# Head norms of both tiles in step, filler products in four waits of TensorE, and the last value tiles of a half evicted by two engines ahead of a weight split

## The reference

```python
h = rmsnorm_2(x, attn_norm)
qkv = h @ w_qkv                       # a: three groups of q, k, v; b: one; 16 heads of 64
q = rope(rmsnorm(q) * q_gain)         # norm over the 64 numbers of a head, for every head
k = rope(rmsnorm(k) * k_gain)
p = exp(q @ k.T * scale + mask - max) # dilated bands in a, causal in b
x = x + (p @ v / sum(p)) @ w_o
hn = rmsnorm_2(x, ffn_norm)
x = x + (silu(conv(hn @ w_gate)) * conv(hn @ w_val)) @ w_down
```

## Time and profile before

| what | value |
|---|---|
| median of 3 runs | 1156.03 us (1153.71 to 1156.86) |
| the profiled execution's own time | 1157.73 us |
| its span in the trace | 1155.9 us |
| PE busy | 1115.3 us, 96% of the span |
| PEld, DVE, ACT, POOL busy | 84%, 68%, 56%, 1% |
| chain that ended last | PE 87%, DVE 6%, ACT 5%, issue 2%, DMA 1% |
| mean DMA rate | 159 GB/s |

### The profile page before, as it was taken

The page is one execution under the profiler, slowest core; times in us unless marked ns, Lnnn a source line. Parts: engine busy times, 40 slices in busy tenths (PEclk is TensorE's granted clock), DMA queues, the critical chain, the costliest instruction groups (busy, mean ns, idle before and its releaser), DMA issues.

```text
span 1155.9 us, 19015 instructions
## 1 busy us (share of the span) xinstructions
PE 1115.3 (96%) x6928; PEld 969.3 (84%) x6928; DVE 788.3 (68%) x1435; ACT 646.7 (56%) x1122; POOL 12.9 (1%) x22
## 2 busy tenths in 40 slices
PE   7998789999998999999999999999999999999998
PEld 5876679998987887888878999999876769999997
DVE  5767566555557667576674687787874746887776
ACT  5364455454456555655575665555666556655554
POOL 0000100000000000000000000000000000000000
PEclk9997689999999999999999999999999999999999
DMA  9552045655644655046541456556552515565562
GB/s 324 149 182 73 26 132 183 189 182 186 193 147 148 213 180 165 25 147 203 161 146 46 156 184 208 190 168 195 169 177 74 185 56 179 182 199 182 165 203 106
DMA packets 117037, 184.33 MB, mean 159 GB/s; under 512 B 6640, under 2 KB 70384, under 8 KB 116720
## 3 DMA queue, kind: packets, MB, share of 16 engines
q1 hardware_dynamic: 116688, 183.23, 50.0%
q10 hardware_dynamic: 288, 0.29, 0.1%
HBM read 182.45 MB, written 1.05 MB: 159 GB/s over the span
## 4 chain that ended last, share of the span: by engine, by line
PE 87%; DVE 6%; ACT 5%; issue 2%; DMA 1%; SPq 0%; DVEq 0%; ACTq 0%
PE ps L679 10%; PE ps L681 10%; PE ps L680 10%; PE ps L655 10%; PE ps L657 9%; PE ps L656 9%; PE ps L738 5%; PE ps L739 5%; PE ps L740 5%; PE ps L832 2%; PE ps L815 2%; PE ps L797 2%; ACT w_hi L1117 1%; PE ps L858 1%; PE ps L755 1%
## 5 line engine op out<-in xcount | busy, mean ns | idle before, releaser
L1624 DVE TENSOR_TENSOR w_lo<-w_stage,w_hi 128x1024 fp32r<-128x1024 f32 x336 | 403.1, 1222 | 191.3 <-ACT w_hi L1117 190.4
L1117 ACT ACTIVATE w_hi<-w_stage 128x1024 fp32r<-128x1024 f32 x336 | 347.7, 1053 | 182.7 <-PE ps L657 86.6
L679 PE MATMUL ps<-aT_hi,w_hi 128*128 128x256 f32 x992 | 282.2, 284 | 0.7 <-DVE aT_lo L1638 0.7
L680 PE MATMUL ps<-aT_lo,w_hi 128*128 128x256 f32 x992 | 281.2, 283 | 0.0
L681 PE MATMUL ps<-aT_hi,w_lo 128*128 128x256 f32 x992 | 281.2, 283 | 0.0
L655 PE MATMUL ps<-w_hi,aT_hi 128*128 128x512 f32 x480 | 194.2, 405 | 3.9 <-DVE w_lo L1697 2.2
L679 PEld LDWEIGHTS ps<-aT_hi,w_hi 128*128 128x128 f32 x992 | 190.8, 192 | 2.3 <-issue 1.0
L680 PEld LDWEIGHTS ps<-aT_lo,w_hi 128*128 128x128 f32 x992 | 190.9, 192 | 1.0
L681 PEld LDWEIGHTS ps<-aT_hi,w_lo 128*128 128x128 f32 x992 | 190.8, 192 | 0.0
L657 PE MATMUL ps<-w_hi,aT_lo 128*128 128x512 f32 x480 | 190.1, 396 | 0.0
L656 PE MATMUL ps<-w_lo,aT_hi 128*128 128x512 f32 x480 | 190.0, 396 | 0.0
(11 more groups left out here) (220 smaller groups left out, 1165.9 us busy)
## 6 DMA issues: line engine op xcount, KB each, us to landing
w_stage<-in_ffn_w_up SPq DMA_DIRECT2D x88, 512.0 KB, 4.7
w_stage<-in_a_w_qkv SPq DMA_DIRECT2D x72, 512.0 KB, 4.1
w_stage<-in_ffn_w_down SPq DMA_DIRECT2D x44, 512.0 KB, 3.5
w_stage<-in_w_up SPq DMA_DIRECT2D x32, 512.0 KB, 3.8
w_stage<-in_w_down SPq DMA_DIRECT2D x32, 512.0 KB, 4.2
w_stage<-in_w_in SPq DMA_DIRECT2D x24, 512.0 KB, 4.7
w_stage<-in_b_w_qkv SPq DMA_DIRECT2D x24, 512.0 KB, 4.5
w_stage<-in_w_out SPq DMA_DIRECT2D x8, 512.0 KB, 3.8
```

What stands on the lines that cost most here:

```text
L679: pe.matmul(o, wh, aT_hi[:, k, :], start=(k == 0), stop=False)
L680: pe.matmul(o, wh, aT_lo[:, k, :], start=False, stop=False)
L1117: act.activation(w_hi[:, slot, :], w_in[:, slot, :], ACT.Copy).then_inc(hi_done[slot], 1)
L1624: dve.tensor_tensor(w_lo[:, slot, :], w_in[:, slot, :], w_hi[:, slot, :].bitcast(F32), ALU.subtract).then_inc(lo_done[slot], 1)
```

## The change

Three parts.

- `head_norms` is split in two. ACT squares both token tiles back to back (`head_squares`), with the fourth split of the quarter group behind the squares, and then takes one Ln and one Exp over 16 columns for both tiles (`head_scales`). DVE sums both (`head_means`) and later scales and rotates both (`rotated_heads`). On ACT both norms now stand ahead of the eviction of q. On DVE split 7 moves behind the rotations of k. On PE the transposes of k in the last group stand behind v tile 3 instead of 4, and v tiles 6 and 7 behind the scores of unit 1.
- `spin` issues plain fp32 products of 128 by 128 columns into a bank that is written anew afterwards: 8 on a tile of zeros and 2 and 10 on the identity around the first transposes, 13 at the end of `mix`, 16 and 10 ahead of the two late `turn_x`. POOL clears the tile of zeros first.
- At the end of a half ACT takes the exponentials of unit 1 and evicts v's token tile 0 ahead of split 11, DVE evicts token tile 1 ahead of its split 11.

```diff
...
+            def spin(n, o, m):
+                for _ in range(n):
+                    pe.matmul(o, m, m, start=True, stop=True)
+            pe.wait_ge(s["zeroed"], 1)
+            spin(8, ps[:, 3, 0:P], hid[:, 0, 0:P])
             pe.wait_ge(s["ident_in"], 16)
             for ks in (LOW, HIGH):
                 for t in range(TOK):
                     turn_x("norm_in1", in_ready, t, ks)
+                    if (t, ks) == (0, LOW):
+                        spin(2, ps[:, 3, 0:P], ident)
+            spin(10, ps[:, 3, 0:P], ident)
...
+            pe.wait_ge(*is_drained(S_, f"sA{2 * NH1 - 1}"))
+            spin(13, ps[:, 0, 0:P], ident)
             pe.wait_ge(s["osq"], at(S_, "osq", 3))
...
             last_rows(S_, 4, "r3", 1, range(5, KT))
+            spin(16, ps[:, 7, 0:P], ident)
             turn_x("norm_mlp", ready, 1, LOW)
...
             last_down(S_, 0, range(4), ((1, 1),), True)
+            spin(10, ps[:, 7, S:2 * S].rearrange("p (r t c) -> p r t c", t=TOK, c=8)[:, :, 1, :], ident)
             turn_x("norm_a", ready, 1, LOW, "in")
...
-                        dense_rows(S_, 0, n + 8, v, tiles=range(KT - 3))
+                        dense_rows(S_, 0, n + 8, v, tiles=range(KT - 4))
                         turn_heads(S_, (f"kt{g}0", f"kt{g}1"), 0, 4 * g + 4)
-                        dense_rows(S_, 0, n + 8, v, tiles=[KT - 3])
+                        dense_rows(S_, 0, n + 8, v, tiles=[KT - 4])
                         for nm in (f"kt{g}0", f"kt{g}1"):
                             pe.wait_ge(*is_drained(S_, nm))
-                        for u in range(2):
-                            scores(S_, units[u], u)
-                            dense_rows(S_, 0, n + 8, v, tiles=[KT - 2 + u])
+                        scores(S_, units[0], 0)
+                        dense_rows(S_, 0, n + 8, v, tiles=[KT - 3])
+                        scores(S_, units[1], 1)
+                        dense_rows(S_, 0, n + 8, v, tiles=range(KT - 2, KT))
...
-                def head_norms(names):
+                def head_squares(names):
...
-                        act.wait_ge(s["ms8"], at(S_, "ms8", n[0], i))
-                        rsqrt(stat(f"rs8{t}", 8), stat(f"ms8{t}", 8), stat(f"ln8{t}", 8), "rs8")
+                def head_scales():
+                    act.wait_ge(s["ms8"], at(S_, "ms8", n[0], i))
+                    rsqrt(stat("rs8", 16), stat("ms8", 16), stat("ln8", 16), "rs8")
                 for g in range(groups):
                     q0 = g * 12
-                    splits(S_, range(q0, q0 + 4), i)
-                    head_norms((f"q{g}0", f"q{g}1"))
-                    splits(S_, range(q0 + 4, q0 + 8), i)
+                    splits(S_, range(q0, q0 + 3), i)
+                    head_squares((f"q{g}0", f"q{g}1"))
+                    split(S_, q0 + 3, i)
+                    head_scales()
+                    splits(S_, range(q0 + 4, q0 + 7), i)
+                    head_squares((f"k{g}0", f"k{g}1"))
+                    split(S_, q0 + 7, i)
+                    head_scales()
                     for j in range(2):
                         evac_q(...)
-                    head_norms((f"k{g}0", f"k{g}1"))
...
                     if last:
                         split(S_, q0 + 10)
                         exps(S_, units[0], 0)
-                    splits(S_, range(q0 + 11, q0 + 12), i)
-                    for t in range(TOK):
-                        evac_v(S_, f"v{g}{t}", i, vv[:, t, g * 512:(g + 1) * 512], stat("rtok", 2)[:, t:t + 1])
+                        exps(S_, units[1], 1)
+                        evac_v(S_, f"v{g}0", i, vv[:, 0, g * 512:(g + 1) * 512], stat("rtok", 2)[:, 0:1])
+                        split(S_, q0 + 11)
...
             def _(pool):
+            pool.memset(hid[:, 0, :], 0.0).then_inc(s["zeroed"], 1)
...
             def project_heads(S_, i, groups, layer, units):      # DVE
...
-                    splits(S_, range(q0, q0 + 4), i)
+                    splits(S_, range(q0, q0 + 3), i)
+                    head_means((f"q{g}0", f"q{g}1"))
+                    split(S_, q0 + 3, i)
...
-                    head_norms((f"q{g}0", f"q{g}1"), 0, (layer * 3 + g) * 2)
-                    splits(S_, range(q0 + 4, q0 + 8), i)
+                    rotated_heads((f"q{g}0", f"q{g}1"), (layer * 3 + g) * 2)
+                    splits(S_, range(q0 + 4, q0 + 7), i)
+                    head_means((f"k{g}0", f"k{g}1"))
                     for j in range(2):
                         dve.wait_ge(*is_full(S_, f"qt{g}{j}", i))
-                    head_norms((f"k{g}0", f"k{g}1"), 1, (layer * 3 + g) * 2 + 1)
+                    rotated_heads((f"k{g}0", f"k{g}1"), (layer * 3 + g) * 2 + 1)
+                    split(S_, q0 + 7, i)
...
                 maxima(S_, units[1], 1)
+                last = f"v{groups - 1}1"
+                b = bank(S_, last)
+                dve.wait_ge(*is_full(S_, last))
+                dve.tensor_scalar(vv[:, 1, (groups - 1) * 512:groups * 512], ps[:, b, :], stat("rtok", 2)[:, 1:2], None,
+                                  ALU.mult).then_inc(drained[b], 1)
                 split(S_, q0 + 11)
```

More of the change, by code:

```diff
@@ L257, in make_plan @@
     halves_a = [Stage(f"half_a{n}", uses=proj_a + attention_uses(8), quarters=q_a,
-                      counts={"sq": 12, "ms8": 12, "rs8": 12, "rot": 12, "act_step": 12, "dve_step": 12,
+                      counts={"sq": 12, "ms8": 12, "rs8": 6, "rot": 12, "act_step": 6, "dve_step": 12,
                               **ATTENTION_COUNTS}) for n in range(2)]
@@ L263, in make_plan @@
                       quarters=[None] * 3 + ["q01"] + [None] * 3 + ["k01"] + [None] * 3 + ["v01"],
-                      counts={"sq": 4, "ms8": 4, "rs8": 4, "rot": 4, "act_step": 4, "dve_step": 4,
+                      counts={"sq": 4, "ms8": 4, "rs8": 2, "rot": 4, "act_step": 2, "dve_step": 4,
                               **ATTENTION_COUNTS})
@@ L414, in blocks_kernel @@
             "orstd", "osq", "sq", "ms8", "rs8", "silu", "u", "uhi", "ulo", "msq", "pms", "prstd", "x_new",
-            "lam", "const_ready", "gate_w", "unit", "rd", "bc", "ohi", "olo")}
+            "lam", "zeroed", "const_ready", "gate_w", "unit", "rd", "bc", "ohi", "olo")}
         def is_full(stg, name, i=0):
@@ L1446, in project_heads @@
                         exps(S_, units[0], 0)
-                    splits(S_, range(q0 + 11, q0 + 12), i)
-                    for t in range(TOK):
-                        evac_v(S_, f"v{g}{t}", i, vv[:, t, g * 512:(g + 1) * 512], stat("rtok", 2)[:, t:t + 1])
+                        exps(S_, units[1], 1)
+                        evac_v(S_, f"v{g}0", i, vv[:, 0, g * 512:(g + 1) * 512], stat("rtok", 2)[:, 0:1])
+                        split(S_, q0 + 11)
+                    else:
+                        split(S_, q0 + 11)
+                        for t in range(TOK):
+                            evac_v(S_, f"v{g}{t}", i, vv[:, t, g * 512:(g + 1) * 512], stat("rtok", 2)[:, t:t + 1])
             def ffn(tag, layer):
@@ L1555, in _ @@
                 project_heads(S_, 0, NG, 0, units)
-                exps(S_, units[1], 1)
                 attention(S_, units)
@@ L2028, in project_heads, with head_means, rotated_heads @@
                 n = [0]
-                def head_norms(names, which, j):
+                def head_means(names):
                     for t in range(TOK):
                         dve.wait_ge(s["sq"], at(S_, "sq", n[0] + 1, i))
-                        dve.tensor_reduce(stat(f"ms8{t}", 8), sqb[:, t, :].rearrange("p (h d) -> p h d", d=HD),
+                        dve.tensor_reduce(stat("ms8", 16)[:, 8 * t:8 * t + 8],
+                                          sqb[:, t, :].rearrange("p (h d) -> p h d", d=HD),
                                           AX.X, ALU.add).then_inc(s["ms8"], 1)
                         n[0] += 1
-                        dve.wait_ge(s["rs8"], at(S_, "rs8", n[0], i))
+                def rotated_heads(names, j):
+                    dve.wait_ge(s["rs8"], at(S_, "rs8", n[0] // 2, i))
+                    for t in range(TOK):
                         b = bank(S_, names[t])
@@ L2040, in head_norms @@
                                                  scalar=stat("rtok", 2)[:, t:t + 1],
-                                                 in1=stat(f"rs8{t}", 8).unsqueeze(2).broadcast_to([P, 8, HD]),
+                                                 in1=stat("rs8", 16)[:, 8 * t:8 * t + 8].unsqueeze(2)
+                                                 .broadcast_to([P, 8, HD]),
                                                  op0=ALU.mult, op1=ALU.mult).then_inc(drained[b], 1)
```

## The result

The median of six runs is 1147.43 us (1146.09 to 1150.34) against 1156.44 for the kernel before, ratio 0.9926 with a 95% interval of 0.9907 to 0.9944: faster, by less than one per cent but clear of the noise. That is 9.0 us where 8.0 were forecast and 1148.0 was named. The profiled execution took 1147.94 with a span of 1146.1.

What follows compares the result with a forecast made beforehand. PE, working through nearly all of the span, was taken to bound the kernel. The halves' 3.5 us plus the fillers' 4.5 made 8.0, taken off the median of 1156.0 to give 1148.0 us; range 1141.0 to 1152.6.

Steps and rivals of the forecast that it cites:

- Head norms in step: In all four halves, PE's 1.00 us wait for the rotated keys goes: 3.9 us.
- Value tiles ahead of split 11: End of each half: PE's wait for v goes or shrinks, but about 1.4 us for DVE's copy of bank 5 appears.
- parts one and three: Head norms and value tiles in the four halves, summed as 2 x 0.65 + 2 x 1.1 = 3.5 us; bounds 0 and 9.0.
- The price of a filler: Fillers in PE's waits: 0.15 us apiece at most at full clock, 0.23 at half, delaying PE by 0.1 at most.
- One sign of being wrong: In the first 30 us, L655 waiting for w_lo would mean that the weights bound the start.
- What the fillers bring: Start 2.2, end of mix 1.0, out1 0.3, mlp_tail 1.0: 4.5 us; bounds 0 and 9.3.
- the fillers bring all: Rival on all filler places: 3.5 + 9.3 = 12.8 us saved, giving 1143.2; chance 0.12.
- The sum: Whole kernel: 3.5 + 4.5 = 8.0 us off the median of 1156.0, giving 1148.0; chance 0.52.
- Nothing changes: Rival, whole kernel: fillers bring nothing and the waits only change their names, 1156.0; chance 0.05.
- fillers bring nothing: Rival on the filler places: the clock rises and falls where it did, 1152.5; chance 0.15.
- Cleared of waits: Rival at the halves' ends: no bank 5 wait takes over, 9.0 us and the slow stretch at 928 go, 1141.0; chance 0.13.
- The slower case: Rival in the four halves: late reload behind DVE's split 7 makes ACT wait for a DMA, 1159.5; chance 0.03.

## Why the prediction was right, and where it was not

- **Head norms in step** went as worked out: no wait at L858 in any half, k ready ahead of PE. Alone beside the fillers it shortens a half by 1.2 us (21.86 to 20.67 and 19.60 to 18.37), 4.8 in all, more than the 3.9 of the waits: ACT's last splits and evictions move up with it.
- **Value tiles ahead of split 11.** The new wait was foreseen with its cause and size (1.4 forecast, 1.34 measured in a, 1.35 in b), and moving the split showed the cause. What the sum hid is the sign. The step said that ACT starts split 10 "at 456.1, as before, because the saved wait is taken by the scores that now precede tile 5", and counted parts one and three as one term of 3.5 us. Rightly so for the pair, 2.8 by the distances; but that sentence says that this part takes back what part one gives. Costed by itself, with part one already in, it is a loss of 0.76 us in a half of a and 0.31 in one of b.
- **The price of a filler** was mis-sized: "0.15 apiece at most" and "0.23 apiece" at half clock. The rows read count records, and a product has two: x4 in 0.60 us were two products. Measured: 0.23 and 0.43. Hence "they delay PE by 0.1 us at most" failed in mix, where 13 products took 5.13 us in a wait of 3.35 and PE came 1.4 late; the forecast's sign that o_sb would be transposed at the same distance behind DVE as before did not hold.
- **The wait at the start.** One sign of being wrong did appear: L655 waits 1.32 us for `w_lo` at 11.48. It does not bear the meaning given to it, that the weights bound the start. The wait was 2.22 before and ends 0.1 us earlier now; some of it stayed because the last transposes of x (twelve records) took 1.53 us instead of 2.82 and PE came to the fillers earlier, and L655 waits for `w_lo` nowhere else before 40 us.
- **What the fillers bring.** 4.5 forecast; 5.0 alone, 9.3 on top of the change's edits of the halves, 5 to 8 with the last split moved as well. That 9.3 is the upper bound of the forecast's own sum for them, the size that the rival "the fillers bring all" had, while the halves without them bring nothing. The start was 2.2 forecast and 2.7 measured, and the choice to go by the durations and not by the clock column was right. The Trainium skill (TensorE: Matmul & The Clock Gate, section "What's actually happening") has half rate as the state in which the engine begins, and the traces agree with it: the last twelve records of x's transposes take 2.82 us in the kernel before and 1.53 behind the first fillers. Out1 and mlp_tail were mis-sized: 1.3 forecast, 4 to 5 measured. Of the 1.0 for mix no run tells the share by itself; start and mix beside the halves' edits give 4.3 us by the medians (5.0 by the ratios), which leaves 1.5 to 2.1 for mix if the start's share adds. The forecast also left out two stretches of mix that its windows didn't show, 88.7 to 95.5 and 102.3 to 105.7, 10.2 of the 47.8 us at 1.2 GHz; as much is left there after (three of 3.4 us, from 87.3, 97.6 and 107.8).
- **The sum** failed in form, not in size: it adds the terms. The halves' 3.5 stood for any state of the fillers, and without them they are worth nothing; the 2.8 us by distance were there in the same trace, and the clock took 1.7 of them in one stretch. That 1148.0 lies 0.6 from the measured 1147.4 is in part luck: the halves were put 0.7 too high, the places of the fillers too low, and the filler's price at half.
- **The rivals.** "Nothing changes" and "fillers bring nothing" fell with the fillers alone. "Cleared of waits", forecast at 1141.0, is what the kernel is once the last split is moved (1139.5). The slower case, a DMA behind split 7, didn't come: ACT waits for no DMA at the end of any half. A slower end existed and was none of the rivals: value tiles without the head norms, 1160.6.

## What to carry to other kernels

Move a step in a hand-written order one at a time on paper and give each its own sign: here two edits together gained 2.8 us in the halves, and one of them alone gained 4.8. When a wait gives way to one for another engine's copy, look at what stands ahead of that copy on its list; work that nobody needs soon, here the last split, can go behind it, and that was worth 7.9 us on top of the change's 9.0. A short wait of PE costs its length and, in these traces, 1.7 us more for each stretch of 1.2 GHz that follows it; so the gains of edits that shift such waits don't add, and a change must be timed with the others in place.

## What the runs showed of the hardware that was not expected

A fall of the granted clock came at the same place in two profiles of one kernel (874.57 and 874.30, both just behind the wait of 1.35 us), and not in the kernel after, which has the same wait at 866.6 and 0.44 for the product behind it. What decides between the two isn't shown by these runs. The number of low stretches at 870 and 925 also differed with no difference in the work there (none and one in the profile after, two and two without the fillers of out1 and mlp_tail), but the second of these is the slowest of seven executions, so the removed fillers aren't shown to be the reason. The kernels with no wait over 0.5 us left at the end of a half had no such stretch there in any of their three profiles, nor had the kernel with the copy ahead of the maxima, whose longest wait there is 0.93.

The clock column misses half rate at the start: in the kernel before it reads 1.00 from 11.58 to 16.83 while products are 0.44 us apart. In the kernel with the last split later and no fillers column and durations agree there (0.60 from 12 to 16).
